# Two-layer hybrid attention trunk: blocks of a task turned in equal groups, turns and values one step later behind the scores

## What is computed

```python
def dense_causal_attention(q, k, v, scale, cum_log_forget=None):
    ...
    def one_block(i):                       # 128 queries
        logits = jnp.einsum('bqhd,bkhd->bhqk', qb, k, ...) * scale
        if cum_k is not None:
            logits = logits + cq[..., None] - cum_k[:, :, None, :]
        logits = jnp.where(s_pos[None, :] <= t[:, None], logits, NEG_INF)
        p = jax.nn.softmax(logits, axis=-1)
        return jnp.einsum('bhqk,bkhd->bqhd', p.astype(v.dtype), v)
...
def nsa_attention(...):
    # cmp: 63 compressed keys; sel: top-k blocks of 64 keys; win: the last 512 keys
    return gb[..., 0:1] * o_cmp + gb[..., 1:2] * o_sel + gb[..., 2:3] * o_win
```

## Time and profile before

| | |
|---|---|
| median of 3 runs | 2976.65 us |
| time of the profiled execution | 2973.8 us |
| its span, first to last instruction | 2972.0 us |
| TensorE busy | 2841.2 us, 96% of the span |
| TensorE weight loads | 2311.2 us, 78% |
| VectorE / ScalarE / GpSimd busy | 1141.2 / 827.4 / 923.0 us |
| mean granted TensorE clock | 0.985 |

### The profile page before, as it was taken

The page is one execution under the profiler, slowest core; times in us unless marked ns, Lnnn a source line. Parts: engine busy times, 40 slices in busy tenths (PEclk is TensorE's granted clock), DMA queues, the critical chain, the costliest instruction groups (busy, mean ns, idle before and its releaser), DMA issues.

```text
span 2972.0 us, 36478 instructions
## 1 busy us (share of the span) xinstructions
PE 2841.2 (96%) x13804; PEld 2311.2 (78%) x13804; DVE 1141.2 (38%) x1837; ACT 827.4 (28%) x1455; POOL 923.0 (31%) x610
## 2 busy tenths in 40 slices
PE   8998899989999999999999999888899999999998
PEld 4796888868888888886778777677688888888867
DVE  3425878233222222225433434675522222222254
ACT  3304777331110001114321222675501110000250
POOL 2321155323233332334222223213333332333432
PEclk9999999999999999999999999799999999999999
DMA  4456633211111111111242313643011111111112
GB/s 156 140 182 229 163 86 79 93 35 43 50 50 49 43 49 49 49 63 37 72 173 96 34 42 38 142 115 118 29 50 50 42 49 49 49 48 44 64 36 78
DMA packets 105220, 227.79 MB, mean 77 GB/s; under 512 B 41379, under 2 KB 53155, under 8 KB 104791
## 3 DMA queue, kind: packets, MB, share of 16 engines
q1 hardware_dynamic: 93224, 181.91, 22.2%
q10 hardware_dynamic: 11872, 44.21, 3.8%
HBM read 188.36 MB, written 41.39 MB: 77 GB/s over the span
## 4 chain that ended last, share of the span: by engine, by line
PE 86%; DVE 8%; issue 2%; ACT 2%; DMA 1%; SPq 0%; POOL 0%; ACTq 0%; DVEq 0%; POOLq 0%
PE ACC L1302 65%; PE ACC L1599 5%; PE TR L1535 3%; PE OP L1568 3%; PE ACC L1521 3%; PE OP L1411 2%; PE ACC L1392 2%; DVE XL L2114 1%; DVE H L2134 1%; DVE T L2131 1%; DVE PT L2345 1%; DVE PB L2324 1%; ACT PT L1900 1%; PE ACC L1494 1%; DVE M L2163 0%
## 5 line engine op out<-in xcount | busy, mean ns | idle before, releaser
L1108 POOL CAST WH<-RAW 128x1024 fp32r<-128x1024 f32 x188 | 197.8, 1052 | 1426.1 <-PE ACC L1302 1373.4
L1302 PE MATMUL ACC<-XH,WH 128*128 128x512 f32 x1728 | 552.3, 401 | 32.7 <-DVE XL L2114 26.1
L1302 PE MATMUL ACC<-XL,WH 128*128 128x512 f32 x1728 | 534.2, 390 | 0.0
L1302 PE MATMUL ACC<-XH,WL 128*128 128x512 f32 x1728 | 533.5, 390 | 0.0
L1110 POOL TENSOR_TENSOR WL<-RAW,WH 128x1024 fp32r<-128x1024 f32 x188 | 453.0, 2410 | 21.5
L1302 PEld LDWEIGHTS ACC<-XH,WH 128*128 128x128 f32 x1728 | 323.9, 188 | 127.9 <-issue 53.4
L1853 ACT ACTIVATE HH<-T 128x1024 fp32r<-128x1024 f32 x64 | 68.0, 1062 | 1149.9 <-DVE T L2156 1149.9
L1302 PEld LDWEIGHTS ACC<-XH,WL 128*128 128x128 f32 x1728 | 325.2, 188 | 68.6
L1302 PEld LDWEIGHTS ACC<-XL,WH 128*128 128x128 f32 x1728 | 325.2, 188 | 68.4
L2163 DVE TENSOR_TENSOR M<-M,ACC 128x1024 f32<-128x1024 f32 x128 | 156.3, 1221 | 481.9 <-PE ACC L1302 479.7
L1302 PE MATMUL ACC<-HH,WH 128*128 128x512 f32 x1024 | 316.6, 390 | 3.3 <-DVE M L2163 3.1
(11 more groups left out here) (251 smaller groups left out, 3477.5 us busy)
## 6 DMA issues: line engine op xcount, KB each, us to landing
RAW<-in_w SPq DMA_DIRECT2D x203, 512.0 KB, 3.5
QK<-y_odds SPq DMA_DIRECT2D x56, 256.0 KB, 5.8
QK<-y_foxs SPq DMA_DIRECT2D x48, 256.0 KB, 5.6
y_foxs<-HALVES ACTq DMA_DIRECT2D x8, 1024.0 KB, 4.9
y_foxv<-HALVES ACTq DMA_DIRECT2D x4, 1024.0 KB, 4.5
BIAS<-y_f SPq DMA_DIRECT2D x8, 512.0 KB, 7.5
H<-in_xT ACTq DMA_DIRECT2D x8, 512.0 KB, 6.4
y_h<-H ACTq DMA_DIRECT2D x8, 512.0 KB, 2.7
```

Source lines behind the costliest of these rows:

```text
L1108: nc.gpsimd.tensor_copy(WH[:, slot], RAW[:, slot]).then_inc(s_whi, 1)
L1302: mm = nc.tensor.matmul(acc[:, h * HALF:(h + 1) * HALF], w(k), x[:, k, h * HALF:(h + 1) * HALF], start=first and k == k0 and w is ws and x ...
```

## The change

`TURN_LAG` goes from 2 to 3 and `VALUE_LAG` from 5 to 6 for fox, mla, cmp, sel and win; the dilated tasks keep a turn lag of 2 (`SMALL_LAG`) and their value lag of 3. A task of more than four blocks is turned in two equal groups, the first rounded up, where it was four blocks and the rest: five blocks are 3 + 2 (they were 4 + 1), six are 3 + 3 (4 + 2); seven and eight stay at 4 + 3 and 4 + 4. The values of the job `win` of pair 0 are turned through the TR ring in its first step and no longer through unused parts of ACC.

```diff
-TURN_LAG, VALUE_LAG, DILATED_LAG = 2, 5, 3
+TURN_LAG, SMALL_LAG, VALUE_LAG, DILATED_LAG = 3, 2, 6, 3
...
-            if kind in ("sel", "win") and (kind, pair) != ("sel", 0):
-                j.values = "kept" if pair else "spare"
+            if kind in ("sel", "win") and pair:
+                j.values = "kept"
...
+        def turned_at(s):
+            t = get(s - SMALL_LAG)
+            if t and t.kind in DILATED:
+                return t
+            t = get(s - TURN_LAG)
+            return t if t and t.kind not in DILATED else None
...
-            st.logits, st.turn, st.values, st.norm, st.out, st.start = get(s), get(s - TURN_LAG), None, None, None, None
+            st.logits, st.turn, st.values, st.norm, st.out, st.start = get(s), turned_at(s), None, None, None, None
...
             if st.turn:
-                for g0 in range(0, len(st.turn.blocks), 4):
-                    st.turn.groups.append(group(g0, min(4, len(st.turn.blocks) - g0), whole=st.turn.kind in DILATED))
+                n = len(st.turn.blocks)
+                size = (n + 1) // 2 if n > 4 else n
+                for g0 in range(0, n, size):
+                    st.turn.groups.append(group(g0, min(size, n - g0), whole=st.turn.kind in DILATED))
```

## The result

The changed kernel takes 3007.7 us (median of 8 runs) where the kernel before, beside it, takes 2976.5. The ratio is 1.0082, with a 95% interval of 1.006 to 1.0103: slower by 24 us (the two medians differ by 31) and outside the predicted range. The profiled execution took 3007.6 us, its span is 3005.8 us, with TensorE busy for 2866.6 us at a mean granted clock of 0.975 (2972.0 us, 2841.2 and 0.985 before). In the experiments the times of both kernels proved to lie in two groups some 14 us apart, of which the three runs known before showed only one. That is why the two figures, 24 and 31, differ so much: five of seven times after lie in the upper group, and one of eight before.

A forecast was written before the change was run, and what follows sets the result against it. TensorE's work or waits bound the kernel, the change acting on some 55 us of attention idle time; 4.5 + 6.5 + 0.3 + 1.8 - 0.5 - 1.2 = 11.4 us on 2976.65 gave 2988.0 us, range 2975 to 2997.

The forecast's parts named there:

- what bounds the attention: Nearly all idle time of the turns is the TR bank's loop; VectorE's chain sets turn 2 to turn 5, 5.63 us.
- Rival 1: Attention turns wait for the exponential after all, so the longer lag makes the kernel faster: 2958 us; chance 0.15.
- Rival 2: No difference: growth in stretches taken as full of TensorE work is absorbed, leaving 3.4 us, 2980 us; chance 0.13.
- D: Turn 7 to the next head's turn 2, full of TensorE work: +0.34 us per fox head, +0.52 per mla head.
- A: Turn 2 to turn 5 of a head, set by VectorE: +0.13 us in fox, +0.25 in mla.
- C: Turn 6 to turn 7, set by the TR bank's loop: stays 2.10 us; in win 0.34 us less.
- B: Turn 5 to turn 6, full of TensorE work: +0.09 us per fox head, +0.12 per mla head.
- Sel: Sel heads, with fox's blocks: +0.45 us each (between 0.3 and 0.56), four heads 1.8 us.
- win: Win heads, the one place where equal groups pay: -0.13 us each, four heads -0.5 us.
- the ring: First win job: a 2.8 us wait for values goes, a 1.6 us stall comes; net -1.2 us (bounds -1.5, +0.5).
- The sum of the order's terms: All head, phase-start and first-win-job terms together, over the whole kernel: 11.4 us slower.
- rival 3: Slower still: waits in seven heads let the granted clock fall, costing 10.5 us more, 2998.5 us; chance 0.11.

The follow-up runs named there:

- e1: The changed kernel with the old groups (four blocks and the rest), so the longer lag without equal groups: 3004.2 us, ratio 1.0077.
- e2: The kernel before with equal groups alone, lags as before: 2968.6 us, ratio 0.9966.
- e6: The kernel before with only the values of the first win job turned through the TR ring: ratio 1.001.
- e11: The changed kernel with constant transposes in the wait before turn 5 and in that ahead of the 64-column matmuls: 2987.4 us.
- e5: The changed kernel with eight constant transposes ahead of turn 5 of each fox, mla and sel head: 2986.6 us, ratio 1.0031.
- e10: The changed kernel with ten constant transposes in the wait ahead of the 64-column matmuls; the expected median of 2993 to 2996 us came true.
- e4: The changed kernel with 9 constant transposes added some 25 us ahead of the 64-column matmuls: ratio 1.0043.

## Why the prediction was right and wrong

**Right: what bounds the attention, and the sign.** T(7) did not wait for its exponential: an extra step in between left its wait (0.88 us to 0.77) and the 2.11 us from T(6). Rival 1 (faster) is out, by the profile after and by e1. Rival 2 (absorbed) is out too: D grew.

**A, T(2) to T(5): right with e = 1.** Fox: 5.63 to 5.74 us, forecast +0.13; the wait 1.04 us, forecast 1.10. Mla: 5.64 to 5.89, forecast +0.25. With e = 0 it is +0.25 for fox, twice the forecast, where the multiplication by the inverse sums lies in the chain as well, and +0.3 for mla. The two halves of the term show apart in fox e = 1: 5.87 with the lag alone (e1), 5.50 with the groups alone (e2).

**D, T(7) to T(2'): right in kind, a little high.** Fox 6.64 to 6.91 and 6.26 to 6.62, +0.27 and +0.36, forecast 0.34. Mla 6.87 to 7.31 and 6.72 to 7.23, +0.44 and +0.51, forecast 0.52.

**C: right.** 2.11 us before and after; in win 2.13 to 1.78, forecast -0.34.

**B, T(5) to T(6): mis-sized, and of the wrong sign in half the heads.** I had called it full of TensorE work, + 0.09 and + 0.12. With e = 1, where a turn of the spread sums stands in it, TensorE has no idle time in it, but it grows by 0.01 only: V starts 0.38 us after L(1') and started 0.37 after L(0'), so half of what L(2) has over L(0) was the wrong price. With e = 0 it is 2.13 us before, which is the TR bank's loop again, and the first group of T(5), three blocks for four, shortens it to 1.93: -0.20 (1.94 with the groups alone, e2; 2.13 with the lag alone, e1). The earlier trace rows shows a head with e = 1, 294.22 to 296.59; the other kind had to be read too. So a fox head grew by 0.37 to 0.40 and not 0.56, an mla head by 0.57 to 0.72 and not 0.89.

**Sel, win and the ring: mis-sized.** Between heads without a fall a sel head of pair 1 grew by 0.14 and 0.39, forecast 0.45; a win head by -0.59 (e = 0) and -0.05, forecast -0.13 for each; the ring gave 0.26 (e6), forecast 1.2.

**The sum of the order's terms: too high by some 3 us, and near the times by luck.** 11.4 us were forecast; e11 lies 10.1 us above the kernel before (2987.4 against 2977.3), e5 some 9 (lower groups, 2986 against 2977). But these two still hold falls of the clock which the sum does not: the one behind the 2.9 us wait (2.9 us in e11) and, in their profiled executions, one at the end of the heads (1.2 us). From T(2) of the first even head to T(2) of the last e11's trace is 8.0 us longer than before's, where 10.7 follow from the terms. TensorE's busy time, said to be unchanged, grew from 2841.2 to 2866.6 us with no matmul added: it is longer at the lower clock.

**The step that failed: that the granted clock would be as before, with rival 3 kept apart at 0.11.** Three things were missed. First, within the heads the rival came on top of the forecast and not in its place: e10 less e11 is 6.2 us, from falls in heads with e = 0 (I had said e = 1), in a few heads of each run. Second, the fall behind the 2.9 us wait is in no term. Third, the 13 to 15 us at the 64-column matmuls are in no term and no rival. I read the three runs shown, 2976.4 to 2978.3, as the kernel's spread, and 0.2% as what a measurement can tell; the kernel before is at 2991 in 28 of 77 runs. In the first comparison the step was in 5 of 7 of the changed kernel's runs and 1 of 8 of the others: 0.59 x 14 = 8.2 us. Together 10.1 + 6.2 + 8.2 = 24.5 us, against 24.4 measured. That it closes to 0.1 is chance: the third comes from another comparison than the first two, and like against like the change cost 16.2 and 18.4 us, which with 8.2 gives 24 to 27. The 16 to 18 us are what the change costs; the 8.2 us are how often the step fell on either side in one comparison.

**Open.** Whether the change makes the step more likely. 13 of 19 against 28 of 77 speaks for it; e4 with two runs of four, e5 with four of ten and e1 with one of four (if its three lower times are without the step), all with the long lag, do not. The instructions and the wait ahead of the matmuls are the same in both traces, and the measurements were on different chips. It was not tried further. Open too is why the fall behind the 2.9 us wait comes with the long lag only. That short transposes and the 0.93 us wait bring the step on is shown only so far as filling the wait nearly ends it.

## What to carry to other kernels

Before lengthening a software pipeline, see which engine's chain sets each stretch. A stage more between scores and turn gave TensorE slack, but VectorE runs in order and had to do two longer tasks in its busiest stretch, while the work taken from TensorE there went where TensorE had no slack. The name on a wait is a hint: compare the end of the producer with the start of the consumer before paying for the edge. A kernel whose granted clock can fall in a short wait should be timed in enough runs to see both groups, and idle waits ahead of matmuls that do not raise the clock again are worth filling. A change in one stage can move the clock in another that it does not touch: compare the granted clock stage by stage.

## What the runs showed of the hardware

A run of 128 float32 matmuls of 64 columns takes 14.5 us at full clock. In the six profiled executions with the step it began at full clock, the clock fell 0.9 to 2.4 us after its first matmul, and it took 25.3 to 26.7 us: at 1.2 GHz to its end though TensorE was busy throughout, and back at full clock only in the 512-column matmuls behind. Two waits of 0.7 and 1.0 us shortly behind one another let the clock fall in some heads and not in others of the same execution. Eight constant transposes in the second of them kept it up in every even-layer head of two profiled executions (e5, e11); ten ahead of the 64-column matmuls did in 43 of 46 runs, by their times. Three in each cmp task held 2.4 GHz through a stage that ran at 1.2 in every other trace; it took 32.9 us for 35.2, and the kernel no less.
